# First mixer of a fused two-block model on one core: scores and values in high and low parts, their product in three passes of rounded operands in place of a plain fp32 product

## The reference

```python
scores = jnp.sum(qc[:, :, :, None, :] * kc[:, :, None, :, :] * decay, axis=-1)
intra = jnp.einsum('bhij,bhjv->bhiv', scores, vc)
...
o_f = gla_chunked(qh, kh, vh, la_f, False)
o_b = flip(gla_chunked(flip(qh), flip(kh), flip(vh), flip(la_b), True))
o = (o_f + o_b).transpose(0, 2, 1, 3)
o = rms_norm(o, o_norm_g).reshape(B, S, GLA_V).astype(h.dtype) * jax.nn.silu(g)
return o @ w_out
```

## Time and profile before

| | |
|---|---|
| median of 3 runs | 2163.75 us (2163.63 to 2164.08) |
| the profiled execution | 2163.63 us, span 2161.8 us, granted clock 1.0 |
| PE busy | 2144.5 us, 99% of the span |
| DVE busy | 1680.9 us, 78% |
| ACT busy | 1176.7 us, 54% |
| POOL busy | 253.0 us, 12% |
| the first mixer | about 340 to 600 us of the span |
| its levels | heads 0 to 3 from about 378 us to 560 us |
| its scores x values | 437.2 to about 574.5 us, 8 products of 4 |

### The profile page before, as it was taken

The page is one execution under the profiler, slowest core; times in us unless marked ns, Lnnn a source line. Parts: engine busy times, 40 slices in busy tenths (PEclk is TensorE's granted clock), DMA queues, the critical chain, the costliest instruction groups (busy, mean ns, idle before and its releaser), DMA issues.

```text
span 2161.8 us, 33546 instructions
## 1 busy us (share of the span) xinstructions
PE 2144.5 (99%) x13412; PEld 1835.3 (85%) x13412; DVE 1680.9 (78%) x2546; ACT 1176.7 (54%) x1922; POOL 253.0 (12%) x187
## 2 busy tenths in 40 slices
PE   9999999999999999999999999999999999999999
PEld 6989897777779898989899997777789898977777
DVE  8789697988678796888787787777688886966873
ACT  6536264667556263546355356777555362638672
POOL 3000004000040000040010112000130000030000
PEclk9999999999999999999999999999999999999999
DMA  7454535131135555354554542222135545332211
GB/s 214 123 136 99 151 94 161 40 98 60 46 89 141 124 137 151 84 162 125 176 129 127 122 126 92 77 75 95 50 79 150 137 100 150 98 131 74 79 59 39
DMA packets 249451, 237.75 MB, mean 110 GB/s; under 512 B 4984, under 2 KB 245240, under 8 KB 249296
## 3 DMA queue, kind: packets, MB, share of 16 engines
q1 hardware_dynamic: 208336, 210.25, 30.3%
q0 software_dynamic: 40752, 25.11, 8.7%
q10 hardware_dynamic: 208, 0.24, 0.0%
HBM read 213.79 MB, written 6.32 MB: 102 GB/s over the span
## 4 chain that ended last, share of the span: by engine, by line
PE 91%; DVE 4%; ACT 2%; issue 1%; DMA 0%; SPq 0%; ACTq 0%; DVEq 0%
PE ps L1982 90%; PE ps L1986 1%; DVE sb_wlo L1334 1%; DMA sb_raw<-ffn_w_gu 0%; ACT sb_whi L771 0%; DVE sb_gla_ek L1689 0%; DVE sb_gla_eq L1692 0%; ACT sb_hyb_th L771 0%; ACT sb_lnb L771 0%; DVE sb_gla_cf L1681 0%; DVE sb_gla_xb L1684 0%; DVE sb_gla_d L1669 0%; SPq L737 0%; DVE sb_rb L1965 0%; ACT sb_xh L771 0%
## 5 line engine op out<-in xcount | busy, mean ns | idle before, releaser
L1982 PE MATMUL ps<-sb_xh,sb_whi 128*128 128x512 f32 (+1 forms) x1812 | 625.4, 345 | 3.6 <-issue 1.8
L1982 PE MATMUL ps<-sb_xl,sb_whi 128*128 128x512 f32 (+1 forms) x1812 | 608.8, 337 | 0.1
L1982 PE MATMUL ps<-sb_xh,sb_wlo 128*128 128x512 f32 (+1 forms) x1812 | 606.7, 337 | 0.0
L771 ACT ACTIVATE sb_whi<-sb_raw 128x1024 fp32r<-128x1024 f32 (+1 forms) x368 | 379.9, 1037 | 376.6 <-PE ps L1982 359.8
L1982 PEld LDWEIGHTS ps<-sb_xh,sb_whi 128*128 128x128 f32 x1812 | 344.0, 190 | 56.8 <-issue 20.4
L1982 PEld LDWEIGHTS ps<-sb_xl,sb_whi 128*128 128x128 f32 x1812 | 344.2, 190 | 39.3 <-DVE sb_xl L1354 3.3
L1982 PEld LDWEIGHTS ps<-sb_xh,sb_wlo 128*128 128x128 f32 x1812 | 343.9, 190 | 37.1
L1982 PE MATMUL ps<-sb_ffn_tl,sb_whi 128*128 128x256 f32 x1200 | 339.6, 283 | 0.0
L1982 PE MATMUL ps<-sb_ffn_th,sb_whi 128*128 128x256 f32 x1200 | 339.6, 283 | 0.0
L1982 PE MATMUL ps<-sb_ffn_th,sb_wlo 128*128 128x256 f32 x1200 | 339.6, 283 | 0.0
L1334 DVE TENSOR_TENSOR sb_wlo<-sb_raw,sb_whi 128x1024 fp32r<-128x1024 f32 (+1 forms) x218 | 275.6, 1271 | 49.1 <-ACT sb_whi L771 48.6
(11 more groups left out here) (293 smaller groups left out, 2919.9 us busy)
## 6 DMA issues: line engine op xcount, KB each, us to landing
sb_raw<-ffn_w_gu SPq DMA_DIRECT2D x86, 1024.0 KB, 5.8
sb_raw<-ffn_w_down SPq DMA_DIRECT2D x32, 1024.0 KB, 5.1
sb_raw<-sb_raw POOLq DMA_DIRECT2D x75, 256.0 KB, 4.2
sb_raw<-w_ada SPq DMA_DIRECT2D x12, 1024.0 KB, 7.6
sb_raw<-ffn_w_down SPq DMA_DIRECT2D x16, 768.0 KB, 5.6
sb_raw<-gla_w_in SPq DMA_DIRECT2D x12, 1024.0 KB, 5.5
sb_raw<-diff_w_in SPq DMA_DIRECT2D x12, 1024.0 KB, 5.1
sb_raw<-w_in SPq DMA_DIRECT2D x10, 1024.0 KB, 5.1
```

The source lines that it names most:

```text
L771: return e.activation(out, in_, func, bias=bias, scale=scale)
L1982: return e.matmul(out, lhsT, rhs, start=start, stop=stop, skip_group_check=skip)
```

## The change

The score matrix and the values get a high and a low part, and `("pv", h, d)` becomes the same three passes of rounded operands that the projections use: 12 products of 512 columns in place of 4 plain ones (each of two records).

- The score matrix is no longer double-buffered: its memory holds `at_hi` and `at_lo` (both named `sb_gla_at`), float32r. DVE's masked copies of scores 0 to 7 go to a new double buffer `sb_gla_near` (float32). ACT rounds it into `at_hi` once a head (4 new ACT copies, semaphore `g_dh`) and copies scores 8 and 9 as before, now rounded. DVE makes the low parts (`low_scores`): for score 8 one subtraction of 512 columns (near blocks) and two of 256, in step `("score", h, 9)`; for score 9 two of 512, in step `("score", h+1, 0)`, for head 3 in `("copy", 3, 9)`. These are 5 new DVE instructions a head, 20 in all.
- Values: ACT writes the rounded `sb_gla_v` and then the same 4 pieces again unrounded into one buffer `sb_gla_vw` (8 x 4 new ACT copies), waiting for `g_vlo` of the unit before; DVE subtracts (`low_values`, 8 new instructions of 512 columns, `sb_gla_vl`), one or two levels later.
- A score bank of score 8 or 9 is free only when DVE has made its low part (`g_alo`), not when ACT has copied it (`g_atc`). The products wait for `g_alo` and `g_vlo`, the transposes' bank for 8 instead of 4 value copies.
- The reserved SBUF area grows, and the descriptor memory for DMAs that POOL issues is set to 4096 bytes of a partition.

```diff
@@ -50,7 +50,7 @@
-STAGE = 21792
+STAGE = 24864
@@ -432,6 +432,16 @@
 
+        def near_blocks(a_):
+            return a_.rearrange("p (n c) -> p n c", c=640)[:, :, 0:128]
+
+        def next_blocks(a_, k):
+            off = (128, 512)[k]
+            return a_.rearrange("p (n c) -> p n c", c=1280)[:, :, off:off + 128]
+
+        def far_blocks(a_, g):
+            return a_[:, 0:2048].rearrange("p (n c) -> p n c", c=512)[:, 2 * g:2 * g + 2, (1 - g) * 256:(2 - g) * 256]
+
         def tiles_of(t):
@@ -470,9 +480,11 @@
             ek = [t_(f"ek{i}", [128, S]) for i in range(2)]
-            both = t_("at", [128, 2 * 2048 + 512])
-            at = [both[:, 2048 * i:2048 * i + 2560] for i in range(2)]
-            GV = [t_(f"v{i}", [128, 4, 256]) for i in range(2)]
+            near = [t_(f"near{i}", [128, 4, 128]) for i in range(2)]
+            both = t_("at", [128, 2 * 2048 + 512], F32R)
+            at_hi, at_lo = (both[:, 2048 * i:2048 * i + 2560] for i in range(2))
+            GV, GVL = ([t_(f"{n}{i}", [128, 4, 256], F32R) for i in range(2)] for n in ("v", "vl"))
+            gvw = t_("vw", [128, 4, 128])
             z1, gvt, gro, on = t_("z1", [128, S]), t_("vt", [128, S]), t_("ro", [128, S]), t_("on", [128, S])
@@ -965,6 +977,10 @@
                                 scale=rbcol[:, t:t + 1]).then_inc(sem["g_vrow"], 1)
+                        w.wait_ge(sem["g_vlo"], n)
+                        for t in range(4):
+                            act(gvw[:, t, :], psum[GLA_MISC][:, t * 128:(t + 1) * 128], ACT.Copy,
+                                scale=rbcol[:, t:t + 1]).then_inc(sem["g_vrow"], 1)
                     elif s[0] == "gates":
@@ -1042,21 +1058,18 @@
             def wide_scores(h, i):
-                A = at[h % 2]
                 if i == 8:
-                    wide = A.rearrange("p (n c) -> p n c", c=1280)
                     src = ring_bank("score", h, 8, 0)[:, :].rearrange("p (n e c) -> p n e c", n=2, e=2)
+                    w.wait_ge(sem["g_at"], 8 * h + 8)
+                    w.wait_ge(sem["g_o"], 2 * h)
+                    act(near_blocks(at_hi), near[h % 2][:, :, :], ACT.Copy).then_inc(sem["g_dh"], 1)
                     w.wait_ge(sem["g_level"], 11 * h + 9)
-                    if h >= 2:
-                        w.wait_ge(sem["g_o"], 2 * (h - 1))
-                    for k, off in ((0, 128), (1, 512)):
-                        act(wide[:, :, off:off + 128], src[:, :, k, :], ACT.Copy).then_inc(sem["g_atc"], 1)
+                    for k in range(2):
+                        act(next_blocks(at_hi, k), src[:, :, k, :], ACT.Copy).then_inc(sem["g_atc"], 1)
                 else:
-                    rows = A[:, 0:2048].rearrange("p (n c) -> p n c", c=512)
                     for g in range(2):
                         w.wait_ge(sem["g_level"], 11 * h + 10 + g)
-                        act(rows[:, 2 * g:2 * g + 2, (1 - g) * 256:(2 - g) * 256],
-                            ring_bank("score", h, 9, g)[:, :].rearrange("p (n c) -> p n c", c=256),
+                        act(far_blocks(at_hi, g), ring_bank("score", h, 9, g)[:, :].rearrange("p (n c) -> p n c", c=256),
                             ACT.Copy).then_inc(sem["g_atc"], 1)
@@ -1583,6 +1596,7 @@
                 e.tensor_scalar(neg_b, cols("b_gate"), -1.0, None, ALU.mult).then_inc(sem["negated"], 1)
+                turned_v = None
                 for s in GS:
@@ -1613,6 +1627,18 @@
                         level(*s[1:])
+                        if turned_v is not None:
+                            low_values(turned_v)
+                            turned_v = None
+                    elif s[0] == "vT":
+                        turned_v = s[1]
+                    elif s[0] == "score" and s[2] == 9:
+                        low_scores(s[1], 8)
+                    elif s[0] == "score" and s[1] and s[2] == 0:
+                        low_scores(s[1] - 1, 9)
+                    elif s == ("copy", 3, 9):
+                        low_values(7)
+                        low_scores(3, 9)
                     elif s[0] == "osq" and s[2]:
@@ -1692,14 +1718,37 @@
             def scores(h, i):
-                diag = at[h % 2].rearrange("p (n c) -> p n c", c=640)[:, :, 0:128]
                 m = mask[:, i:i + 1, :].broadcast_to([128, 4, 128])
...
                 if h >= 2:
-                    w.wait_ge(sem["g_o"], 2 * (h - 1))
-                e.copy_predicated(diag, m, ring_bank("score", h, i, 0)[:, :].rearrange(
+                    w.wait_ge(sem["g_dh"], h - 1)
+                e.copy_predicated(near[h % 2][:, :, :], m, ring_bank("score", h, i, 0)[:, :].rearrange(
                     "p (n c) -> p n c", c=128)).then_inc(sem["g_at"], 1)
+
+            def low_scores(h, i):
+                if i == 8:
+                    src = ring_bank("score", h, 8, 0)[:, :].rearrange("p (n e c) -> p n e c", n=2, e=2)
+                    w.wait_ge(sem["g_dh"], h + 1)
+                    w.wait_ge(sem["g_at"], 8 * h + 8)
+                    e.tensor_tensor(near_blocks(at_lo), near[h % 2][:, :, :], near_blocks(at_hi).bitcast(F32),
+                                    ALU.subtract).then_inc(sem["g_alo"], 1)
+                    w.wait_ge(sem["g_atc"], 4 * h + 2)
+                    for k in range(2):
+                        e.tensor_tensor(next_blocks(at_lo, k), src[:, :, k, :], next_blocks(at_hi, k).bitcast(F32),
+                                        ALU.subtract).then_inc(sem["g_alo"], 1)
+                else:
+                    for g in range(2):
+                        w.wait_ge(sem["g_atc"], 4 * h + 3 + g)
+                        e.tensor_tensor(far_blocks(at_lo, g),
+                                        ring_bank("score", h, 9, g)[:, :].rearrange("p (n c) -> p n c", c=256),
+                                        far_blocks(at_hi, g).bitcast(F32), ALU.subtract).then_inc(sem["g_alo"], 1)
+
+            def low_values(n):
+                own = slice((n % 2) * 128, (n % 2 + 1) * 128)
+                w.wait_ge(sem["g_vrow"], 8 * n + 8)
+                e.tensor_tensor(GVL[n // 2 % 2][:, :, own], gvw[:, :, :], GV[n // 2 % 2][:, :, own].bitcast(F32),
+                                ALU.subtract).then_inc(sem["g_vlo"], 1)
 
@@ -2164,7 +2213,7 @@
                 if key[0] == "vT":
-                    w.wait_ge(sem["g_vrow"], 4 * key[1] + 4)
+                    w.wait_ge(sem["g_vrow"], 8 * key[1] + 8)
                 elif key[0] == "oss":
@@ -2226,15 +2275,16 @@
                         _, h, d = s
-                        A = at[h % 2]
-                        w.wait_ge(sem["g_at"], 8 * h + 8)
-                        w.wait_ge(sem["g_atc"], 4 * h + 4)
-                        w.wait_ge(sem["g_vrow"], 4 * (2 * h + d + 1))
+                        w.wait_ge(sem["g_alo"], 5 * h + 5)
+                        w.wait_ge(sem["g_vlo"], 2 * h + d + 1)
                         if h:
                             w.wait_ge(sem["g_on"], 2 * h - 1 + d)
+                        own = slice(d * 128, (d + 1) * 128)
                         for t in range(4):
-                            ins = mm(psum[GLA_O[d]][:, :], GV[h % 2][:, t, d * 128:(d + 1) * 128],
-                                     A[:, t * 512:(t + 1) * 512], t == 0, t == 3)
+                            row = slice(t * 512, (t + 1) * 512)
+                            mm(psum[GLA_O[d]][:, :], GV[h % 2][:, t, own], at_hi[:, row], t == 0, False)
+                            mm(psum[GLA_O[d]][:, :], GV[h % 2][:, t, own], at_lo[:, row], False, False)
+                            ins = mm(psum[GLA_O[d]][:, :], GVL[h % 2][:, t, own], at_hi[:, row], False, t == 3)
                         ins.then_inc(sem["g_o"], 1)
@@ -2247,7 +2297,7 @@
                         else:
-                            w.wait_ge(sem["g_atc"], 16)
+                            w.wait_ge(sem["g_alo"], 20)
                         got[m] = k
@@ -2267,7 +2317,7 @@
                 else:
-                    w.wait_ge(sem["g_atc"], 4 * h + (2 if n == 8 else 4))
+                    w.wait_ge(sem["g_alo"], 5 * h + (3 if n == 8 else 5))
 
@@ -2756,7 +2806,7 @@
     arrays = {k: np.ascontiguousarray(v) for k, v in arrange(**{k: np.asarray(v) for k, v in inputs.items()}).items()}
-    nc = bacc.Bacc("TRN2", target_bir_lowering=False, num_devices=1)
+    nc = bacc.Bacc("TRN2", target_bir_lowering=False, num_devices=1, dynamic_dma_scratch_size=4096)
     args = {k: nc.dram_tensor(k, v.shape, mybir.dt.from_np(v.dtype), kind="ExternalInput").ap()
...
     args["outT"] = nc.dram_tensor("outT", (D, S), F32, kind="ExternalOutput").ap()
```

2 lines of the change are left out of this document (1 added, 1 removed).

## The result

| | before | after |
|---|---|---|
| time, median (range) | 2163.69 (2163.60 to 2164.08) | 2174.97 (2173.03 to 2176.83) |
| profiled execution | 2163.63, span 2161.8 | 2174.71, span 2172.9 |

The ratio of the times is 1.0052, interval 1.0036 to 1.0068. Forecast: 2171.2, range 2166.5 to 2176.5. The sign and the places are as forecast, the size is 3.8 us short.

The account below looks back on a forecast made before the run. PE was taken as the bound (91% of the chain), DVE near its limit at 88%. PE's lateness, waits for DVE less its own saving, came to 7.4 us: 2171.0 profiled, 2171.2 against the median; range 2166.5 to 2176.5, own range 2167.5 to 2175.

Parts of the forecast that it names:

- (a): Gates of head 1: PE waits longer for DVE's masked copy, behind two value subtractions and ACT's delay; +1.5 us.
- (b): Score 9 of head 0: PE waits 2.2 us for three DVE subtractions behind the g unit's copy; lateness 3.7.
- (d): Score 9 of heads 1 and 2: PE waits 3.3 us each for DVE, late by the norm; lateness 5.4, then 7.2.
- (e): Head 3: DVE is 7.3 us late at the last level, PE waits for it, score 9 is 7.3 us late.
- (f): Last products of head 3: PE waits 1.5 us for DVE's subtractions, the pair gives 1.4 back; lateness 7.4.
- PE's saving, 6.1 us: Products of scores and values, all heads: 0.78 us less for six of the eight, 1.4 for the last two together.
- faster: Rival: the waits at score 9 are hidden and PE keeps its 6.1 us, 2157.7; chance 0.04.
- much slower: Rival: DVE bounds from head 0 on, its 14.6 us all paid, none of PE's saving shows, 2178.3; chance 0.08.
- (c): Products of head 0: PE regains 2 x 0.78 us; DVE, 5.4 us late at its masked copy, is just absorbed.
- DVE's work: All heads: 28 new DVE subtractions for values and scores, 14.6 us, between 9 and 21 us in all.
- DVE at over 95% from 420 to 540: Expected sign in the profile after: DVE busy over 95% of the 420 to 540 us window, 88% before.
- The descriptor memory: POOL's smaller memory for DMA descriptors: costed at nothing; if it bound, the feed-forward parts would show it.

Follow-up runs that it names:

- The first experiment: The changed kernel with DVE making the low parts of score 8 before the g unit's copy in every head: 2169.35 us, 1.0025 of before.
- the eleventh run: The changed kernel, all work kept: score 8 and 9 low parts moved earlier, value unit 1's subtraction later, passes on low scores last: 2167.06 us, 1.0016 of before.
- the seventh run: The changed kernel with each product's four passes on the low scores put last, behind the other eight: 2173.54 us, 1.0048 of before.

## Why the prediction was right in its sign and places, and short in its size

The measured lateness of PE (after less before, by the rows), beside the ledger of the prediction:

| step | place | forecast | measured |
|---|---|---|---|
| (a) | gates of head 1, 416.14 to 417.66 | 1.5 | 1.5 |
| (b) | score 9 of head 0, 420.05 to 425.48 | 3.7 | 5.4 |
| (d) | score 9 of head 1, 470.37 to 477.68 | 5.4 | 7.3 |
| (e) | score 9 of head 3, 560.27 to 571.01 | 7.3 | 10.7 |
| (f) | norm's sum, 577.20 to 588.22 | 7.4 | 11.0 |

**PE's saving, 6.1 us.** A pass costs 0.228 us on scores too, as I took it, but a product is 2.81 and not 2.74 us, 0.71 less each, some 0.4 us in six; the last two give 1.3 and not 1.4. So 5.6 us is what the passes save on PE. By themselves they bring 4.1 us of time, since in head 3 DVE binds and PE waits 1.35 us more there. The forecast is not hurt by that, because its step (e) has PE wait for DVE in head 3 anyway; but its rival "faster", at 2157.7, should have stood at 2159.6.

**(a)** Right to the tenth: 1.5 us, through DVE's 0.60 twice and ACT's delay. Taking the value work away brings the old 0.78 us back.

**(b) and (d), the waits.** Forecast 2.2, 3.3 and 3.3 us; measured 2.14, 3.03 and 3.03. The first experiment shows the mechanism of (b), the queue behind the g copy, by its removal. For (d), "DVE is late by the norm" names a part: 1.3 us of the 3.03 are left when the subtractions pass the weight's low part and the g copy, and none when they pass the norm too, but then PE waits elsewhere.

**The step that failed** is the one from the waits to the time: after each wait the sum takes PE up again at full pace, 0.228 us a pass, and has no term for the clock. In the changed kernel the clock is at its lower level for some 3.3 us behind (a) and as long behind head 2's (d); the stretches cost 1.6 us (the half unit behind the gates ends that much later than it would at 0.228 us a pass) and 1.75 (head 3's first score is 10.95 us late, where head 2's score 9 was 9.2). The ledger shows it: the first is in (b)'s difference of 1.7 and (d)'s of 1.9, the second comes between (d) and (e). With the 0.4 us of smaller saving this makes 3.75 us, about what the forecast lacks. Filling the waits keeps the clock at 1.00; the last norm's sum then starts 2.5 us earlier, not 3.35, since PE waits longer for DVE in head 3, and 2.0 us of the median go. The rows of before could not show it: PE's longest wait in these stages is the 0.98 us above. That the measured 2174.97 lies inside the range is in part luck: my own range ends at 2175, and the rest of the stated range up to 2176.5 was drawn for "much slower", not for a lower clock.

**(c)** Right: the lateness of DVE was absorbed, 0.29 us of slack are left of 3.42.

**(e) and (f)** DVE without a gap carries the lateness through head 3, and the last products wait 1.45 us for DVE's subtractions (1.5 forecast). Putting the low passes last takes that wait away.

**DVE's work.** Forecast 28 operations of 14.6 us; DVE has 15.3 us more. One sign of the forecast didn't come: "DVE at over 95% from 420 to 540" was 88%, since the waits of (b) and (d) hold DVE up too. The rival "much slower", all of DVE's work paid and nothing of PE's saving seen, was given 0.08, with 2178.3. All low parts together cost 15.4 us over the passes alone, nearly their whole DVE time, but that the two sums are one thing is not so: the 15.4 hold some 3 us of low clock, and in the eleventh run the same work costs 2167.06 - 2159.56 = 7.5 us. About half of the 15.4 is thus what the low parts cost by the order, the lower clock behind the waits included. Why the other half stays is in part shown: in the eleventh run DVE is busy in 34.21 of 35 us from 540 us on, and PE waits for it.

**The descriptor memory** costs nothing, as forecast.

## What to carry to other kernels

Where a second engine is 88% busy beside the bound, look for each piece of work that it is given at what stands before it and who waits behind it, before counting the first engine's gain. Here 14.6 us of DVE work turned a saving of 4.1 us into a loss: it cost 15.4 us in the first order and 7.5 in the best. So put a subtraction that frees a bank ahead of whatever on its engine waits for PE, and of long operations that can wait: that one move gave 5.6 us. Moving it further only moved the wait. For a wait of 2 us or more added to PE, price what PE does behind it at the lower clock as well, as a risk and not as a certainty.

## What the runs showed of the hardware that I had not expected

- PE's clock goes down behind waits of 2 to 3 us in the midst of dense work: 0.51 in 418 to 420 us after 2.30 us of idle. It stays down for some 3.3 us, which costs 1.6 to 1.75. It doesn't do so each time: 2.14 us (head 0, score 9) and 3.03 us (head 1) were not followed by it, and 2.25 and 2.26 us in two nearly equal kernels once not and once so; over all profiles it was 17 of 27 waits from 1.97 us up. Behind waits of 0.8 to 1.7 us it was not seen in these stages. What decides it stays open. Work that nobody uses, put into the waits, kept it up, and the median fell by 2.0 us, with ranges that touch.
- A POOL subtraction of 512 columns (1.39 us in the mean) held DVE: 1.20 us for an addition that takes 0.42, and 6.1 us in all for eight of them.
- A pass whose both operands are computed data, scores and values, takes the 0.228 us of a pass on weights: in the seventh run the 24 of the last two products take 5.44 us, from 578.54 to 583.98.
